# ScalarE instead of SyncE sends for the stores of two intermediate results

## What is computed

```
scores = einsum('thpd,hpkd->thpk', qp, sub_keys)
s_top, i_top = top_k(scores, 16)                  # twice, then top 16 of the sums
idx  = the 128 experts of each token;  gate = softmax(best)
h    = gelu(einsum('lkd,ld->lk', expert_u[idx], x))
out  = einsum('lk,lkd->ld', gate * h, expert_v[idx])
```

## Time and profile before

| | us |
|---|---|
| median of 3 runs | 3538.93 (3534.08 to 3541.27) |
| profiled execution, its own time | 3541.71 |
| its span, first to last instruction | 3539.9 |
| PE busy | 3338.2 |
| DVE busy | 2672.7 |
| ACT busy | 1400.4 |
| POOL busy | 1031.9 |

### The profile page before, as it was taken

The page is one execution under the profiler, slowest core; times in us unless marked ns, Lnnn a source line. Parts: engine busy times, 40 slices in busy tenths (PEclk is TensorE's granted clock), DMA queues, the critical chain, the costliest instruction groups (busy, mean ns, idle before and its releaser), DMA issues. The chain is left out here.

```text
span 3539.9 us, 46446 instructions
## 1 busy us (share of the span) xinstructions
PE 3338.2 (94%) x18703; PEld 2946.8 (83%) x18703; DVE 2672.7 (76%) x4561; ACT 1400.4 (40%) x1899; POOL 1031.9 (29%) x652
## 2 busy tenths in 40 slices
PE   8997899999999998999999899889999999999998
PEld 7967558889999898788887786789999898888887
DVE  4458654349999895788888497549999896788888
ACT  4322452233333574233333345333333575333333
POOL 6516700002444330333332000002443331333332
PEclk9998999999999999999999899899999999999999
DMA  6313313237898899899997120226888899999996
GB/s 227 108 51 140 109 54 119 90 99 263 301 326 306 297 345 326 321 359 360 363 360 276 54 72 7 84 73 240 313 314 311 290 349 326 350 362 359 360 361 248
DMA packets 330506, 855.56 MB, mean 242 GB/s; under 512 B 22258, under 2 KB 188066, under 8 KB 297139
## 3 DMA queue, kind: packets, MB, share of 16 engines
q1 hardware_dynamic: 256562, 584.12, 47.1%
q0 software_dynamic: 73728, 268.47, 20.7%
HBM read 746.58 MB, written 105.93 MB: 241 GB/s over the span
## 5 line engine op out<-in xcount | busy, mean ns | idle before, releaser
L293 PE MATMUL ps<-ht_hi,parts 128*128 128x384 f32 (+2 forms) x5088 | 1373.8, 348 | 38.5 <-DVE parts L276 38.1
L276 DVE TENSOR_TENSOR parts<-ring,parts 128x2048 fp32r<-128x2048 f32 (+1 forms) x317 | 741.9, 2340 | 357.0 <-ACT parts L268 356.7
L293 PEld LDWEIGHTS ps<-ht_hi,parts 128*128 128x128 f32 x5088 | 936.6, 191 | 85.7 <-DVE parts L276 48.9
L268 ACT ACTIVATE parts<-ring 128x2048 fp32r<-128x2048 f32 (+1 forms) x317 | 606.7, 1914 | 831.7 <-PE ps L1525 677.2
L293 PE MATMUL ps<-ht_lo,parts 128*128 128x384 f32 (+2 forms) x2544 | 877.5, 345 | 0.0
L1888 POOL DMA_INDIRECT scr<-in_p_rows_u,cst x256 | 403.3, 1575 | 885.9 <-DVE scr L1758 563.9
L335 ACT ACTIVATE scr<-ps 128x384 f32<-128x384 f32 (+2 forms) x497 | 244.4, 505 | 942.0 <-PE ps L293 879.6
L1888 POOL DMA_INDIRECT scr<-in_peer_v,cst x256 | 375.3, 1466 | 770.2 <-DVE xres L1775 620.3
L1525 PE MATMUL ps<-parts,ht_lo 128*128 128x512 f32 x2304 | 530.2, 390 | 6.5 <-DVE ht_lo L1852 6.5
L1525 PE MATMUL ps<-parts,ht_hi 128*128 128x512 f32 x2304 | 529.3, 390 | 4.5 <-DVE ht_hi L1852 4.5
L1525 PEld LDWEIGHTS ps<-parts,ht_lo 128*128 128x128 f32 x2304 | 434.4, 189 | 97.3 <-DVE ht_lo L1852 6.9
(11 more groups left out here) (255 smaller groups left out, 2787.4 us busy)
## 6 DMA issues: line engine op xcount, KB each, us to landing
ring<-in_peer_u SPq DMA_DIRECT2D x128, 1024.0 KB, 6.8
ring<-in_peer_v SPq DMA_DIRECT2D x128, 1024.0 KB, 7.5
hbuf<-scr SPq DMA_DIRECT2D x128, 384.0 KB, 7.0
gbuf<-scr SPq DMA_DIRECT2D x96, 512.0 KB, 8.6
scr<-gbuf SPq DMA_DIRECT2D x64, 768.0 KB, 9.3
scr<-hbuf SPq DMA_DIRECT2D x64, 768.0 KB, 11.9
ring<-in_w_in SPq DMA_DIRECT2D x35, 1024.0 KB, 5.4
xres<-in_w_ada SPq DMA_DIRECT2D x18, 1024.0 KB, 7.4
```

Source lines behind the costliest of these rows:

```text
L268: e.activation(halves(m)[0], slot_view(m)[:, 0:units[m][0]], ACT.Copy).then_inc(A.sem, A.up(("hi", m)))
L276: e.tensor_tensor(lo, slot_view(m)[:, 0:units[m][0]], hi.bitcast(F32), ALU.subtract).then_inc(V.sem, V.up(("lo", m), ("slot", m)))
L293: ins = e.matmul(ps, l, r, start=(i == 0), stop=(i == n - 1))
```

## The change

Both functions are called from ScalarE's program instead of SyncE's. A unit's product is sent for ahead of the split_hi and Gelu of the next unit, so behind the Gelu of its second half. The stores of spread gates stand behind the evictions of the steps S4, S5, S8, S9 and so on. The waits inside `keep` and `store`, their semaphores, sizes and addresses are unchanged; what they wait for is now the issuing engine's own count.

```diff
@@ Peer.sp
                 for kind, a, b, _ in order:
                     if kind == "up":
-                        if b == 0 and a:
-                            self.keep(e, w, a - 1)
                         if b == (1 if a in late else 0):
                             load(e, w, U[tag + "u", a] + R + 1)
                         if (a, b) == (NU - 3, 0):
                             self.fetch(e, w, 0)
-                    if kind == "spread" and a >= 4 and a % 4 < 2:
-                        self.store(e, w, a // 4 - 1, 2 * (a % 4))
-                        self.store(e, w, a // 4 - 1, 2 * (a % 4) + 1)
-                self.keep(e, w, NU - 1)
                 w.wait_ge(*self.pt("dotted", SLOTS - 1))
@@ Peer.act
                 for kind, a, b, _ in order:
                     if kind == "up":
+                        if b == 0 and a:
+                            self.keep(e, w, a - 1)
                         self.up_act(e, w, a, b)
...
                     if kind == "spread" and a < STEPS:
                         self.spread_act(e, w, a)
+                    if kind == "spread" and a >= 4 and a % 4 < 2:
+                        self.store(e, w, a // 4 - 1, 2 * (a % 4))
+                        self.store(e, w, a // 4 - 1, 2 * (a % 4) + 1)
+                self.keep(e, w, NU - 1)
                 w.wait_ge(*self.pt("dotted", SLOTS - 1))
```

## The result

The changed kernel takes 3591.2 us (median of 4 runs, 3587.0 to 3595.1) against 3536.5 us for the kernel before in the same comparison: ratio 1.0156, 95% interval 1.0133 to 1.0179. It is slower by 55 us; 3578 was forecast.

What follows compares the result with a forecast made beforehand. PE was busy for 94% of the span, but in the spreading stretch DVE's time was the kernel's. 3541.7 + 4 + 32 + 2 + 1 = 3581, which lies 2.8 us above the median of the runs, so 3578 us; range 3528 to 3620.

Steps and rivals of the forecast that it cites:

- Choosing stages: First part of each layer's up phase: keeps on ScalarE delay split_hi, mostly hidden; +4 us (0 to 9).
- Spreading stages: Second part of each up phase: held stores and keeps delay split_hi, for which DVE waits; 16 us a layer, +32.
- The price of a place: Spreading stages: a pair of stores and a keep before split_hi cost 5.4 us, half way between 2.37 clear and 8.4 loaded.
- the half that was taken back: Spreading stages: half of 31 us a layer removed, since a longer stage gives the DMA engines more time; 16 left.
- seven places and three fourfold stores: Each spreading stage: seven split_hi behind a pair and a keep, 20 us; three times four stores together, 8 us.
- The end of the stage: End of spreading stages: ScalarE held by four stores, PE stalls of 6 and 6.5 us replace 4.6 and 6.1; +2 us.
- The +1 behind the last keep: Behind the last up unit: its keep, 0.45 us, delays the ScalarE step DVE and PE wait for; +1 for two layers.
- A: Sends stay cheap on ScalarE, nothing added in spreading stages, up to 14 us back at their end; 3529 us, chance 0.22.
- B: A send costs ScalarE all it cost SyncE, or the two senders hold each other; 3621 us, chance 0.12.
- C: No measurable change: places hidden, the gain at the stage's end paying for the rest; 3532 to 3546 us, chance 0.14.
- D: DMAs from both engines go through one queue, so only who is held changes; 3621 us, chance 0.03.
- The break-even of 0.7 us: Mean send of a store on ScalarE: below about 0.7 us the kernel gets faster, above it slower.

Runs made afterwards that it cites:

- e9: Changed kernel with every send one place later on ScalarE, the keep behind split_hi of the next unit; 3578.3 us, ratio 1.0107 to the kernel before.
- e1: Kernel before with only the keeps (hbuf) sent for by ScalarE, the stores staying with SyncE; 3543.3 us, ratio 1.0008.
- e2: Kernel before with only the stores (gbuf) sent for by ScalarE, the keeps staying with SyncE; 3576.3 us, ratio 1.0099.
- e6: Changed kernel with each store in 128 pieces of 4 KB instead of 1024 of 512 bytes; 3528.9 us, ratio 0.9975 to the kernel before.
- e5: Changed kernel with one store behind each of four steps instead of two behind each of the first two; 3577.9 us, ratio 1.0107 to the kernel before.
- e8: Kernel before with keeps on ScalarE, stores on SyncE, the last group's four behind the load of the last up unit; 3528.2 us, ratio 0.9967.
- e4: Kernel before, all sends with SyncE, the last group's four stores behind the load of the last up unit; 3525.8 us, ratio 0.9959.

## Why the prediction was right

**Choosing stages: +4 forecast, 3 measured**, 1.2 and 1.6 us, and 0.1 and -1.0 with the keeps alone on ScalarE; single traces don't resolve such amounts. All 43 keeps of a stage took 0.33 to 0.36 us on ScalarE.

**Spreading stages: +32 forecast, +41 measured** (19.7 and 21.0 us among the one-hots instead of 16 each). The mechanism held: sends that are held in front of split_hi, the DMA engines no longer full, VectorE waiting, for 19 and 20 us more where some 15 were forecast. SyncE's loads took 0.33 us. The waits for landings, which got no price, stayed small: 6.2 and 1.0 us against 3.8 and 1.2.

The size within this term owes something to luck. The price of a place was half way between the clear and the loaded queue, 5.4 us for a pair and a keep, and the place shown above cost 1.22 + 1.45 + 2.92 = 5.6; but it is one of the dearer ones. Of the fifteen times a stage in which a pair and then a keep were sent for, the mean was 4.0 us in the first layer and 4.3 in the second, from 1.3 to 9.8. So this price was too high. Against it stands the half that was taken back for a longer stage, which was too much: of the 31 us that the places add up to, 20 came, so that a third was to be taken back, and the total hold fell only by a fifth (48 stores and 21 keeps held ScalarE for 83 and 85 us against 102 and 103 for SyncE). The two errors work against each other. That only seven places and three fourfold stores cost VectorE time isn't shown either: e9 has shown that a hold elsewhere reaches split_hi too.

**The end of the stage: +2 forecast, +12 measured.** This is the term that was most wrong. PE ran dry 16 us behind the last one-hot, as forecast. The four sends took 11.5 us and not 9.3, and they began 7.7 us behind the last one-hot and not 6.1 (second layer; 8.5 in the first), because ScalarE's last evictions came out later. So the stall became 9.4 and 11.3 us instead of 6 and 6.5. That PE would stand one unit earlier was right.

**The +1 behind the last keep** is there: the first matmul of the down phase waits 2.77 us in both layers after the change, against 2.25 before it, 1.0 us for two layers. It is 2.77 in e1 too, where ScalarE has the keeps alone, and 2.25 in e2, where SyncE has them.

**Sum:** 3 + 41 + 12 = 56 against a span that grew by 52.3; the down phases and the stages in front of the first layer vary by 1 to 2 us from trace to trace. The point lay 13 us low, inside the range; every term but the first was too small or just right, so no large errors cancelled between the terms.

**The rivals.** A (sends stay cheap) was wrong for 512-byte pieces and is right for 4 KB pieces: e6 is 3529, the very number that A gave, by the way that A gave (no loss among the one-hots, 14 us less at the ends). B's price wasn't reached, and its second reason, that the senders hold each other, is refuted by SyncE's loads and by e1's keeps, both at 0.33 us. C was wrong, 55 us against no change. D was wrong: there are two queues. The break-even of 0.7 us for the mean send of a store holds as far as it was tried: 1.0 and 1.2 us was slower, 0.75 and 0.8 (e5, but with waits for landings) was slower, 0.5 (e6) faster.

The rule of the Trainium skill ("DMA: Bandwidth & Descriptors", Issuing engines are not separate DMA queues) is that several senders save only the time of sending. These runs agree: with the second sender alone changed, the kernel never got faster than noise (e1 1.0008, e8 the time of e4). Its "usually small" doesn't hold here: with 512-byte pieces the time of sending was 103 us of a stage of 233, and who had to bear it decided whether it cost anything. The same page of the Trainium skill (Queues, rings and completion order) gives SyncE and ScalarE a ring each on every DMA engine; the trace agrees as far as it shows two queues, q10 beside q1.

## What to carry to other kernels

The time that a transfer cost its sender here was not the bare send but the wait for room in its queue. So before sends are moved to a compute engine, add up how long the present sender is held in that stage (SPq pieces of the timeline) and compare it with the new engine's free time and with the slack in front of each step that others wait for. If the holds are long, make the pieces larger first; then it hardly mattered here who sends (0.9975 with ScalarE, 0.9981 with SyncE). And look in the old queue for what stands *behind* a long hold: here one load moved in front of four stores was worth 15 us, and no choice of sender gave more.

## What the hardware showed beyond the expected

- A queue fills by pieces, not by bytes: the last four stores of 512 KB in 512-byte pieces held the sender for 9.3 to 14.2 us (all runs, both layers), the same in 4 KB pieces for 2.2 to 2.8 us.
- 32 fetches of 768 KB a layer in 1536 pieces of 512 bytes instead of 128 of 6 KB cost the down phases nothing that shows (533.2 and 523.5 against 533.4 and 523.5 us), though the DMA engines were near full there (share 0.92 and 0.93 after the change, 0.96 in e6).
- ScalarE's sends run beside its own running instruction: the send at 2930.82 starts 0.45 us after the start of an eviction that lasts 1.12 us. Sends that aren't held cost ScalarE next to nothing: with 128 keeps moved to it the ratio is 1.0008 (0.9999 to 1.0017, e1).
